# An encoder layer on one core: the middle LayerNorm moved beside the gate's first block, the last LayerNorm rewritten for VectorE

## The chip, the cores and the metric

The kernel runs on one core of a Trainium2 chip. A core has five engines that run side by side and wait for each other through semaphores: PE (TensorE, matrix products), DVE (VectorE), ACT (ScalarE), POOL (GpSimd) and SP (SyncE, which here only issues transfers). The metric is the device time of one execution in microseconds. Three executions of the kernel before took 2086.29, 2087.13 and 2090.3 us; the median is 2087.13 us.

## The reference

One layer for 384 tokens (256 of a prompt, 8 x 16 of running streams), model width 2048, all in fp32. Cut to what matters here:

```python
def layer_norm(x, g, b):
    mu = mean(x, -1); var = mean(square(x - mu), -1)
    return (x - mu) * rsqrt(var + 1e-5) * g + b

x = layer_norm(x, ln_in_g, ln_in_b)
mix = concat(forgetting attention, 8 heads; gated delta rule, 8 heads) @ w_out      # 2048 x 2048
x = layer_norm(2 ** 0.25 * x + mix, ln_mix_g, ln_mix_b)                             # the middle LayerNorm
ffn = (silu(x @ w_gate) * (x @ w_up)) @ w_down                                      # d_ff = 5632
y = layer_norm(2 ** 0.25 * x + ffn, ln_ffn_g, ln_ffn_b)                             # the final LayerNorm
```

Outputs are y and the new states of the heads.

## The kernel before, in words

**Tiles.** The 384 tokens are three row tiles of 128 (`TT = 3`). The residual stream `x_res` holds [128 tokens, 3 tiles, 2048]. For a product, PE needs it transposed and split: `aT_hi` and `aT_lo` ([128 channels, 16 channel groups, 384 tokens]) hold a value rounded to fp32r and the rest.

**Weight pieces.** All weights pass in pieces of [128, 512], numbered `g` through the whole program. SP loads a piece to one of 8 slots of `raw`; ACT copies it to `w_hi` (L226), DVE subtracts and gives `w_lo` (L231). These two are rings of 4: a split of piece g waits until PE has used piece g - 4 (`w_used`). A product (`gemm`, L244) takes, for each piece, three tiles of tokens and for each tile three matmuls (hi x hi, hi x lo, lo x hi): 9 matmuls of 128x512. `w_used` of a piece comes with its last matmul on tile 2. ACT and DVE work 3 pieces ahead of PE.

**Stages.** Entry LayerNorm; 8 attention heads; 8 delta-rule heads; `w_out` in 8 blocks of 8 pieces; the middle LayerNorm; the FFN in two halves (gate block of 16 pieces, up block of 16 pieces for 6 and then 5 groups of 512 hidden channels, each half followed by 4 down blocks of 24 or 20 pieces); the final LayerNorm. Order is written out by hand, engine by engine. A `Course` lets small work of one stage stand between the pieces of a product.

**The middle LayerNorm before.** DVE adds the last `w_out` block to `x_res` (L1399), takes statistics (L285), moments (L291) and 1/sqrt by three Newton steps on [128, 3] (L265 to L270). Then come 12 rounds, one for each tile of tokens and quarter of 512 channels: ACT normalises (L307), DVE multiplies by g (L315), POOL adds b (L322), PE transposes four 128x128 blocks (L337), ACT copies them from PSUM to `aT_hi` (L348), DVE subtracts for `aT_lo` (L353). g and b are broadcast to all 128 partitions. The rounds go tile by tile, so the gate's first product can start only after all 12.

**The final LayerNorm before.** After the last down block DVE adds it to `x_res` (L1567), takes statistics and moments, and 12 rounds follow on ACT (L307), DVE (L315) and POOL (L322), each followed by a store of 256 KB. Its g and b are loaded to `raw` once all weights are split.

**Delta-rule heads.** In each head PE issues four small products into two banks (`streams`), two before and two after the products of L1060 and L1062; before the second two it waits for the first two (`g_S01_ps`).

## Time and profile before

| | us |
|---|---|
| median of 3 runs (lowest, highest) | 2087.13 (2086.29, 2090.3) |
| profiled execution, its own time | 2089.48 |
| its span, first to last instruction | 2087.8 |
| PE busy | 1963.7 (94%) |
| DVE busy | 1071.0 (51%) |
| ACT busy | 774.2 (37%) |
| POOL busy | 187.5 (9%) |
| mean granted clock of PE | 0.982 |
| share of PE in the chain of waits | 81% |

Engines overlap, so the shares don't add up. A group's line names engine, source line, operation, out<-in, shapes and count, then busy time and the mean of one instruction in ns. A busy PE isn't PE at its peak: matmuls overlap, and one of 128x512 lasts 0.39 us but follows the one before it by 0.227 us. In the chain of waits each piece was released by the one above it, and "issue" is time in which nothing visible was waited for.

### The profile page before, as it was taken

How to read it: one execution, taken by the hardware profiler on the slowest of the kernel's cores; microseconds unless marked ns; L12 is line 12 of the kernel's file. 1: busy time of each engine (PE TensorE's matmuls, PEld its weight loads, DVE VectorE, ACT ScalarE, POOL GpSimd, SP SyncE). 2: the span in 40 equal slices, each digit the busy share in tenths (PEclk: the TensorE clock that was granted, in tenths of full speed). 3: DMA queues.
4: the chain of work that ended last, by engine and by line, in shares of the span. 5: the costliest groups of instructions: out<-in, count | busy, mean ns of one | idle time of the engine just before them, and what ended most of it. 6: DMA issues, size and time to landing. Idle time of an engine off the chain costs nothing.

```text
span 2087.8 us, 32037 instructions
## 1 busy us (share of the span) xinstructions
PE 1963.7 (94%) x9970; PEld 1634.1 (78%) x9970; DVE 1071.0 (51%) x2274; ACT 774.2 (37%) x1538; POOL 187.5 (9%) x263
## 2 busy tenths in 40 slices
PE   2999999999999998989999999999999999999993
PEld 1899998777777777867888888888888888888882
DVE  7355655677777676455444434343333444444445
ACT  3344443444444443334333333333333333333332
POOL 4011110211222210003000000000000000000003
PEclk9899999999999999998999999999999999999997
DMA  5355555333333332342444444433344444443332
GB/s 171 81 141 143 141 149 134 93 93 98 98 98 98 91 95 76 126 157 81 126 122 131 126 126 125 127 125 129 128 127 131 126 125 124 122 131 126 126 121 101
DMA packets 235946, 249.82 MB, mean 120 GB/s; under 512 B 21624, under 2 KB 154720, under 8 KB 234608
## 3 DMA queue, kind: packets, MB, share of 16 engines
q1 hardware_dynamic: 229376, 235.48, 39.6%
q0 software_dynamic: 6512, 13.60, 2.1%
q8 instruction: 32, 0.52, 0.1%
q14 instruction: 26, 0.21, 0.0%
HBM read 237.63 MB, written 11.35 MB: 119 GB/s over the span
## 4 chain that ended last, share of the span: by engine, by line
PE 81%; DVE 10%; issue 4%; ACT 2%; DMA 1%; POOL 1%; DVEq 0%; POOLq 0%; ACTq 0%; SPq 0%
PE bank L244 71%; DVE work_a L1170 2%; DVE w_lo L231 2%; DMA x_res<-in_x_prompt 1%; ACT w_hi L226 1%; PE bank L1008 1%; POOL x_res L322 1%; PE bank L1502 1%; PE bank L1002 1%; PE bank L1028 1%; DVE x_res L315 1%; DVE pol L267 0%; DVE pol L268 0%; PE bank L436 0%; PE bank L1022 0%
## 5 line engine op out<-in xcount | busy, mean ns | idle before, releaser
L231 DVE TENSOR_TENSOR w_lo<-raw,w_hi 128x512 fp32r<-128x512 f32 x848 | 588.1, 700 | 750.8 <-ACT w_hi L226 747.0
L226 ACT ACTIVATE w_hi<-raw 128x512 fp32r<-128x512 f32 x848 | 526.8, 630 | 835.7 <-PE bank L244 835.5
L244 PE MATMUL bank<-w_hi,aT_hi 128*128 128x512 f32 (+1 forms) x1824 | 721.7, 396 | 8.5 <-DVE w_lo L231 5.8
L244 PE MATMUL bank<-w_hi,aT_lo 128*128 128x512 f32 (+1 forms) x1824 | 694.3, 381 | 0.0
L244 PE MATMUL bank<-w_lo,aT_hi 128*128 128x512 f32 (+1 forms) x1824 | 693.2, 380 | 0.0
L244 PEld LDWEIGHTS bank<-w_hi,aT_hi 128*128 128x128 f32 x1824 | 345.2, 189 | 74.9 <-DVE w_lo L231 16.3
L244 PEld LDWEIGHTS bank<-w_hi,aT_lo 128*128 128x128 f32 x1824 | 344.2, 189 | 57.5
L244 PEld LDWEIGHTS bank<-w_lo,aT_hi 128*128 128x128 f32 x1824 | 345.5, 189 | 47.5
L244 PE MATMUL bank<-w_hi,hT_hi 128*128 128x512 f32 x528 | 206.9, 392 | 0.6 <-DVE x_res L1567 0.5
L244 PE MATMUL bank<-w_hi,hT_lo 128*128 128x512 f32 x528 | 205.9, 390 | 0.0
L244 PE MATMUL bank<-w_lo,hT_hi 128*128 128x512 f32 x528 | 205.8, 390 | 0.0
L322 POOL TENSOR_TENSOR x_res<-x_res,raw 128x512 f32<-128x512 f32 x12 | 19.5, 1658 | 1104.7 <-DVE x_res L315 1104.7
L244 PEld LDWEIGHTS bank<-w_hi,hT_hi 128*128 128x128 f32 x528 | 99.2, 188 | 23.1 <-issue 1.7
L244 PEld LDWEIGHTS bank<-w_hi,hT_lo 128*128 128x128 f32 x528 | 99.2, 188 | 20.8
L244 PEld LDWEIGHTS bank<-w_lo,hT_hi 128*128 128x128 f32 x528 | 99.2, 188 | 20.2
L244 PE MATMUL bank<-w_hi,mixT_hi 128*128 128x512 f32 x192 | 78.8, 410 | 4.9 <-DVE x_res L1399 4.4
L337 PE MATMUL bank<-cn,x_res 128*128 128x128 f32 x96 | 26.5, 432 | 55.5 <-POOL x_res L322 34.5
L244 PE MATMUL bank<-w_lo,mixT_hi 128*128 128x512 f32 x192 | 75.7, 394 | 0.0
L244 PE MATMUL bank<-w_hi,mixT_lo 128*128 128x512 f32 x192 | 75.6, 394 | 0.0
L337 PEld LDWEIGHTS bank<-cn,x_res 128*128 128x128 f32 x96 | 17.2, 217 | 64.4 <-issue 43.4
L1170 DVE SCALAR_TENSOR_TENSOR work_a<-early,cw,work_a 128x384 f32<-128x384 f32 x72 | 44.6, 620 | 20.5 <-POOL early L1298 14.1
L1521 DVE TENSOR_TENSOR hT_lo<-bank,hT_hi 128x512 f32 (+1 forms) x33 | 22.8, 692 | 55.8 <-ACT hT_hi L1513 55.8
(298 smaller groups left out, 1634.7 us busy)
## 6 DMA issues: line engine op xcount, KB each, us to landing
raw<-in_ffn_w_gate SPq DMA_DIRECT2D x176, 256.0 KB, 2.7
raw<-in_ffn_w_up SPq DMA_DIRECT2D x176, 256.0 KB, 2.7
raw<-in_ffn_w_down SPq DMA_DIRECT2D x176, 256.0 KB, 3.0
raw<-in_w_in SPq DMA_DIRECT2D x128, 192.0 KB, 2.4
raw<-in_w_in SPq DMA_DIRECT2D x128, 128.0 KB, 2.2
raw<-in_w_in SPq DMA_DIRECT2D x256, 64.0 KB, 2.2
raw<-in_w_out SPq DMA_DIRECT2D x61, 256.0 KB, 3.0
work_b<-in_cache_fox_k POOLq DMA_DIRECT2D x8, 512.0 KB, 4.4
```

Of the source, the lines that this page charges most:

```text
L226: nc.scalar.activation(w_hi[:, g % RING], raw[:, g % RAW], ACT.Copy).then_inc(sem("w_high"), 1)
L231: nc.vector.tensor_tensor(w_lo[:, g % RING], raw[:, g % RAW], w_hi[:, g % RING], ALU.subtract).then_inc(sem("w_split"), 1)
L244: last = nc.tensor.matmul(acc[t][:, 0:width], l[:, k0 + n, t * P:(t + 1) * P], r[:, g % RING, 0:width], start=(n == 0 and j == 0), stop=(n ...
L315: nc.vector.tensor_tensor(x, x, gb[0][:, c], ALU.mult).then_inc(sem("ln_scaled"), 1)
L322: nc.gpsimd.tensor_tensor(x, x, gb[1][:, c], ALU.add).then_inc(sem("ln_done"), 1)
L337: last = nc.tensor.transpose(bank[6 + r % 2][:, k * P:(k + 1) * P], x_res[:, t, c:c + P], ident)
L1002: nc.tensor.matmul(tl(b4, 0), A[:, 0, :], U[:, 0, :], start=True, stop=True)\
L1008: last = nc.tensor.matmul(tl(b6, t), A[:, t, :], U[:, t, :], start=True, stop=True)
L1028: last = nc.tensor.matmul(tl(b7, t + 1), T[:, t, :], Z[:, t, :], start=True, stop=True)
L1170: ins = V.scalar_tensor_tensor(out=out, in0=ext[:, a, :, r:r + NQ], scalar=w, in1=out, op0=ALU.mult, op1=ALU.add)
L1502: ins = nc.tensor.transpose(bank[6 + t % 2][:, k * P:(k + 1) * P], hb[:, t, k * P:(k + 1) * P], ident)
L1521: nc.vector.tensor_tensor(hT_lo[:, ks, cs], four(bank[6 + t % 2]), hT_hi[:, ks, cs], ALU.subtract).then_inc(sem("h_bank"), 1)
```

## The change

Four parts.

1. **Middle LayerNorm.** The last `w_out` block goes tile by tile in its last 4 pieces (`gemm_tiles_last`), and DVE takes the statistics of each tile as it is added. Only `x * rstd + shift` is then done on `x_res` in place, one quarter of channels for all three tiles at a time: ACT tile 0, DVE tiles 1 and 2. PE transposes that, one channel group of 128 (three tiles) at a time (`turn`). After the transpose a channel is a partition, so g and b are one number per partition (`gb1`, a small load of POOL ahead of the heads), and ACT applies them while it reads PSUM (into `xt`). DVE casts to `aT_hi` and subtracts for `aT_lo`. The gate's first product starts as soon as channel group 0 is there; the other 14 transposes stand in it. Ahead of the first transposes PE issues 6 fp32 products of 128x512 whose result nobody reads.
2. **Residual stream.** The FFN's residual needs `x * g + b` in token layout. POOL does it in 24 operations of 128x512 on quarters, spaced 6 pieces apart from piece 20 on. DVE waits for all of them before the first down block.
3. **Final LayerNorm.** The last down block also goes tile by tile in its last 4 pieces. All is on DVE: `(x - mean) * g` for tile 0 as soon as its moments are there, for the other 8 quarters between the Newton steps, then 12 times `x * rstd + b`, each followed by its store. g and b (2 x 1 MB) are loaded into a buffer of their own during the last four down blocks.
4. **Semaphores.** PE waits in `streams` for `g_S2_ps` (the product of L1062) and no longer for `g_S01_ps`; others are merged.

```diff
+        def gemm_tiles_last(pe, g0, pieces, hi, lo, k0, acc, name, block):
+            def product(n, t):
...
+                if t == TT - 1:
+                    last.then_inc(sem("w_used"), 1)
+                elif n == pieces - 1:
+                    last.then_inc(sem(name + "_done"), 1)
+            for n in range(pieces - RING):
+                for t in range(TT):
+                    product(n, t)
+            for t in range(TT):
+                for n in range(pieces - RING, pieces):
+                    product(n, t)
...
-                    streams(0), streams(1).then_inc(sem("g_S01_ps"), 1)
+                    streams(0), streams(1)
...
-                    W("g_S01_ps")
+                    W("g_S2_ps")
...
-                    sp.wait_ge(sem("g_mix"), HEADS + 1)
-                    load_gb(sp, gb, ln_mix_g[0], ln_mix_b[0])
...
+                    for n, v in enumerate((ln_mix_g, ln_mix_b)):
+                        pool.dma_start(gb1[:, n, :], v[0].rearrange("(k p) -> p k", p=P),
+                                       allow_slow_non_contiguous=True).then_inc(sem("gb1_in"), 16)
...
+                    for t in range(TT):
+                        if t == TT - 1:
+                            split_dve(dve, G_UP0, 0)
+                        out_evac(dve, blk, NCB - 1, t, 1.0)
+                        dve.wait_ge(sem("acc_free"), TT * blk + t + 1)
+                        last = row_stats(t, NCB - 1)
...
+            def ln1_pool(pool):
...
+                    for t in range(TT):
+                        x = ln1_quarter(q, t)
+                        pool_wait(pool, sem("w_used"), G_UP0 + X_WHOLE_AT + X_WHOLE_STEP * (2 * TT * q + t))
+                        nc.gpsimd.tensor_tensor(x, x, gbq[:, 0, :], ALU.mult).then_inc(sem("x_times"), 1)
...
+            def ln1_act(act):
+                for n in range(A_ACT):
+                    split_act(act, G_UP0, n)
...
+                ln1_unit_act(act, 0)
+                for k in range(KD):
+                    act.wait_ge(sem("n1_ps"), k + 1)
+                    if k >= 2:
+                        act.wait_ge(sem("n1_low"), k - 1)
+                    nc.scalar.activation(xt[:, k % 2, :], bank[6 + k % 2][:, 0:TOK], ACT.Identity,
+                                         scale=gb1[:, 0, k:k + 1], bias=gb1[:, 1, k:k + 1]).then_inc(sem("n1_val"), 1)
+                    if k % 4 == 1 and k // 4 + 1 < QUARTERS:
+                        ln1_unit_act(act, k // 4 + 1)
+                    split_act(act, G_UP0 + A_ACT, k)
...
+                for k in range(KD):
+                    dve.wait_ge(sem("n1_val"), k + 1)
+                    nc.vector.tensor_copy(aT_hi[:, k, :], xt[:, k % 2, :]).then_inc(sem("n1_high"), 1)
+                    dve.wait_ge(sem("n1_high"), k + 1)
+                    nc.vector.tensor_tensor(aT_lo[:, k, :], xt[:, k % 2, :], aT_hi[:, k, :], ALU.subtract)\
+                        .then_inc(sem("n1_low"), 1)
+                    split_dve(dve, G_UP0 + 1, k)
...
+                for _ in range(WARM):
+                    nc.tensor.matmul(bank[5][:, :], ident, cn[:, 0:CW], start=True, stop=True)
+                turn(0), turn(1)
+                gemm(pe, G_UP0, NP_IN, aT_hi, aT_lo, 0, CW, ACC, "acc", BLK_MIX, between=Course(turns()),
+                     ready=lambda n: pe.wait_ge(sem("n1_low"), n + 1))
...
+                dve.wait_ge(sem("x_whole"), ROUNDS)
...
+                    if c == 1:
+                        sp.wait_ge(sem("h_ps"), TT * (FB[0] + FB[1]))
+                        load_gb(sp, (gb_last[:, 0, :], gb_last[:, 1, :]), ln_ffn_g[0], ln_ffn_b[0])
...
+                for t in range(TT):
+                    down_evac(dve, 1, c, t, blk)
+                    dve.wait_ge(sem("acc_free"), TT * blk + t + 1)
+                    link(dve, row_stats(t, c))
+                    link(dve, nc.vector.bn_aggr(moments[:, t, :], stats[:, t].rearrange("p a b -> p (a b)")))
+                    if t == 0:
+                        for _ in range(QUARTERS):
+                            centre(*next(units))
...
+                for r in range(ROUNDS):
+                    t, x, cs = quarter(r)
+                    dve.wait_ge(sem("y_centred"), r + 1)
+                    nc.vector.scalar_tensor_tensor(out=x, in0=x, scalar=rstd[:, t:t + 1], in1=gb_last[:, 1, cs],
+                                                   op0=ALU.mult, op1=ALU.add).then_inc(sem("y_whole"), 1)
```

On PE, between the last `w_out` product (`mixT` operands) and the gate's first (`aT` operands), the kernel before has 12 rounds of four transposes (`cn` holds the identity), of which these are the last two:

```order
L337 MATMUL bank<-cn,x_res 128x128 [waits x_low,ln_done]
L337 MATMUL bank<-cn,x_res 128x128 x3
L337 MATMUL bank<-cn,x_res 128x128 [waits x_low,ln_done]
L337 MATMUL bank<-cn,x_res 128x128 x3
```

The changed kernel has there, on the same engine:

```order
L1570 MATMUL bank<-cn 128x512 x6
L1561 MATMUL bank<-cn,x_res 128x128 [waits n1_unit_dve,n1_unit_act]
L1561 MATMUL bank<-cn,x_res 128x128 x2
L1561 MATMUL bank<-cn,x_res 128x128 [waits n1_unit_dve,n1_unit_act]
L1561 MATMUL bank<-cn,x_res 128x128 x2
L248 MATMUL bank<-w_hi,aT_hi 128x512 [waits acc_free,n1_low,w_split]
L248 MATMUL bank<-w_lo,aT_hi 128x512
L248 MATMUL bank<-w_hi,aT_lo 128x512
```

So 6 transposes stand ahead of the product instead of 48, and each piece of it waits for its own channel group (`n1_low`).

On DVE, in the middle LayerNorm, the kernel before alternates the multiplication by g with the subtraction, and no weight split stands between them:

```order
L315 TENSOR_TENSOR x_res<-x_res,work_a 128x512 [waits ln_unit]
L353 TENSOR_TENSOR aT_lo<-bank,aT_hi 128x4x128 [waits x_high]
L315 TENSOR_TENSOR x_res<-x_res,work_a 128x512 [waits ln_unit]
L353 TENSOR_TENSOR aT_lo<-bank,aT_hi 128x4x128 [waits x_high] x4
L231 TENSOR_TENSOR w_lo<-raw,w_hi 128x512 [waits w_high] x16
```

The changed kernel has this for the first two channel groups and the next quarter (L233 is the weight split):

```order
L1544 CAST aT_hi<-xt 128x384 [waits n1_val]
L1546 TENSOR_TENSOR aT_lo<-xt,aT_hi 128x384 [waits n1_high]
L233 TENSOR_TENSOR w_lo<-raw,w_hi 128x512 [waits w_high]
L1544 CAST aT_hi<-xt 128x384 [waits n1_val]
L1546 TENSOR_TENSOR aT_lo<-xt,aT_hi 128x384 [waits n1_high]
L233 TENSOR_TENSOR w_lo<-raw,w_hi 128x512 [waits w_high]
L1519 TENSOR_SCALAR x_res<-x_res,rstd,shift 128x512 x2
```

Each channel group now brings a cast, a subtraction and one split, and every fourth two normalisations besides.

On DVE at the end of the program, the changed kernel has this between the last splits and the last moments (L1670 adds the block, L1783 is the centring):

```order
L1670 SCALAR_TENSOR_TENSOR x_res<-x_res,bank 128x512 [waits acc_done,gb_in]
L310 BN_STATS stats<-x_res 128x6 [waits acc_free]
L1794 BN_AGGR moments<-stats 128x2 [waits dve_chain]
L1783 SCALAR_TENSOR_TENSOR x_res<-x_res,moments,gb_last 128x512 [waits dve_chain]
L1783 SCALAR_TENSOR_TENSOR x_res<-x_res,moments,gb_last 128x512 x3
L1670 SCALAR_TENSOR_TENSOR x_res<-x_res,bank 128x512 [waits acc_done]
```

Before, the three additions stand together, then the three statistics, then the three moments.

## Rows read from the trace of the kernel before

**Rows 1.** Stretches: us, then busy us and count by engine; PEclk, DMA share, GB/s.
```profile
928.00:957.00 29.00, 13.73 (x50) 9.12 (x50) 25.73 (x44) 15.25 (x24) 19.59 (x12) 0.54 0.03 9
957.00:1350.00 393.00, 393.00 (x1762) 325.52 (x1761) 160.48 (x238) 136.60 (x223) 0.00 (x0) 1.00 0.45 126
2053.00:2088.00 35.00, 0.00 (x0) 0.00 (x0) 23.00 (x31) 8.57 (x12) 19.48 (x12) 0.56 0.23 90
```
**Rows 2.** Chain of waits around the middle LayerNorm: start us, us, what.
```profile
928.63 0.69 DVE x_res L1399
...
931.36 0.52 DVE moments L291 x3
...
934.27 0.82 ACT x_res L307
...
954.39 1.27 POOL x_res L322
...
956.82 33.20 PE bank L244 x144
```
**Rows 3.** Timeline of the `w_out` block's end: start us, us, engine, line, [idle before].
```profile
926.16 0.63 ACT L226 ACTIVATE w_hi<-raw 128x512 fp32r<-128x512 f32 x1 [1.41 <-PE bank L244]
927.77 0.39 PE L244 MATMUL bank<-w_hi,mixT_lo 128*128 128x512 f32 x1
```
**Rows 4.** Timeline of PE at the gate's first product.
```profile
956.47 0.78 PE L244 MATMUL bank<-w_hi,aT_hi 128*128 128x512 f32 x1
```
**Rows 5.** Chain of waits: 145 matmuls, four transposes, an fp32 product of 256 columns.
```profile
1059.91 32.87 PE bank L244 x145
...
1159.48 0.44 PE bank L1502 x4
...
111.56 0.43 PE bank L693 x2
```
**Rows 6.** Groups of DVE and ACT by form: count, busy us, mean ns.
```profile
L231 DVE TENSOR_TENSOR w_lo<-raw,w_hi 128x512 fp32r<-128x512 f32 x848 | 588.1, 700 | 750.8 <-ACT w_hi L226 747.0
L1170 DVE SCALAR_TENSOR_TENSOR work_a<-early,cw,work_a 128x384 f32<-128x384 f32 x72 | 44.6, 620 | 20.5 <-POOL early L1298 14.1
L1211 DVE TENSOR_TENSOR early<-early,cn 128x384 f32<-128x384 f32 x8 | 4.5, 558 | 0.3
L773 DVE TENSOR_SCALAR nrep<-ccache 128x128 f32 x7 | 1.5, 220 | 0.0
L307 ACT ACTIVATE x_res<-x_res,shift,rstd 128x512 f32<-128x512 f32 x36 | 27.3, 803 | 41.4 <-DVE shift L296 41.4
L1084 ACT ACTIVATE work_a<-bank,cw 128x384 f32<-128x384 f32 x24 | 14.0, 582 | 0.0
```
**Rows 7.** Timeline of PE in a delta-rule head.
```profile
418.74 0.39 PE L1062 MATMUL bank<-work_a,ke 128*128 128x128 f32 x2
419.06 0.70 PE L1055 MATMUL bank<-work_b,ke 32*128 32x256 f32 x4
```
**Rows 8.** Chain of waits and timeline at the end of the program.
```profile
2053.69 1.89 DVE stats L285 x3
2052.54 0.39 PE L244 MATMUL bank<-w_hi,hT_lo 128*128 128x512 f32 x1
2059.43 18.02 DVE L315 TENSOR_TENSOR x_res<-x_res,raw 128x512 f32<-128x512 f32 x12 [0.96 <-ACT x_res L307]
2060.30 19.48 POOL L322 TENSOR_TENSOR x_res<-x_res,raw 128x512 f32<-128x512 f32 x12 [1104.65 <-DVE x_res L315]
```
**Rows 9.** A stretch at the end, columns as in rows 1.
```profile
2048.00:2052.00 4.00, 4.00 (x19) 3.33 (x18) 0.39 (x1) 0.00 (x0) 0.00 (x0) 1.00 1.00 416
```
**Rows 10.** DMA issues: count, KB each, median us to landing.
```profile
out<-x_res SPq DMA_DIRECT2D x12, 256.0 KB, 2.3
```
**Rows 11.** Timeline of POOL: a load of 2048 short pieces, and its wait in head 0.
```profile
2.31 1.22 POOL L556 DMA_DIRECT2D wg<-in_w_in  x1
370.56 0.11 POOL L1296 MEMSET early<- 128x9 f32 x1 [38.48 <-ACT early L1082]
```

More of the change, by code:

```diff
@@ L234, in gemm @@
         def gemm(pe, g0, pieces, hi, lo, k0, width, acc, name, block, i=0, per=0, blocks_per=0, between=None,
-                 first=False, ends=True, slot0=0):
+                 first=False, ends=True, slot0=0, ready=None):
             for n in range(pieces):
@@ L239, in gemm @@
                 pe.wait_ge(sem("w_split"), g + per * i + 1)
+                if ready is not None:
+                    ready(n)
                 for t in range(TT):
@@ L254, in gemm @@
                 between.upto(None)
+        def gemm_tiles_last(pe, g0, pieces, hi, lo, k0, acc, name, block):
+            def product(n, t):
+                g = g0 + n
+                pe.wait_ge(sem("w_split"), g + 1)
+                if n == 0:
+                    pe.wait_ge(sem(name + "_free"), TT * (block - 1) + t + 1)
+                for j, (l, r) in enumerate(((hi, w_hi), (hi, w_lo), (lo, w_hi))):
+                    last = nc.tensor.matmul(acc[t][:, :], l[:, k0 + n, t * P:(t + 1) * P], r[:, g % RING, :],
+                                            start=(n == 0 and j == 0), stop=(n == pieces - 1 and j == 2))
+                if t == TT - 1:
[8 more added lines that the diff above has]
+                    product(n, t)
         def wait_acc(eng, name, block, t, g_end):
@@ L1383, in gdn_stage_act @@
                         split_act(act, G_OUT_FOX + A_ACT, n)
-                    with act.Fori(0, NCB) as c:
+                    with act.Fori(0, NCB - 1) as c:
                         for n in range(NP_HALF):
                             split_act(act, G_OUT_GDN + A_ACT, n, c, NP_HALF)
+                    for n in range(NP_HALF - A_ACT):
+                        split_act(act, G_OUT_LAST + A_ACT, n)
                 def stats_of_block(dve, c, acc_free):
@@ L1416, in gdn_stage_dve @@
                                 out_evac(dve, 2 * HEADS + c, c, t, ALPHA)
-                    with dve.Fori(0, NCB) as c:
+                    with dve.Fori(0, NCB - 1) as c:
                         for n in range(NP_HALF):
@@ L1421, in gdn_stage_dve @@
                             out_evac(dve, 2 * HEADS + NCB + c, c, t, 1.0)
-                        stats_of_block(dve, c, TT * (2 * HEADS + NCB + 1 + c)).then_inc(sem("x_stats"), 1)
-                    dve.wait_ge(sem("x_stats"), NCB)
+                        stats_of_block(dve, c, TT * (2 * HEADS + NCB + 1 + c))
+                    for n in range(NP_HALF - A_DVE):
+                        split_dve(dve, G_OUT_LAST + A_DVE, n)
+                    blk = 2 * HEADS + 2 * NCB - 1
+                    for t in range(TT):
[4 more added lines that the diff above has]
+                        last = row_stats(t, NCB - 1)
+                    link(dve, last)
                 def gdn_stage_pe(pe):
@@ L1468, in encoder_layer, with ln1_quarter @@
             hT_lo = sb(ctx, "hT_lo", [P, KH, TOK], F32R)
-            sg = sb(ctx, "sg", [P, TT, CW])
-            hb = sb(ctx, "hb", [P, TT, CW])
+            with ExitStack() as hidden:
+                sg = sb(hidden, "sg", [P, TT, CW])
+                hb = sb(hidden, "hb", [P, TT, CW])
+                xt = sb(hidden, "xt", [P, 2, TOK])
+                gbq = sb(hidden, "gbq", [P, 2, CW])
+            gb_last = sb(ctx, "gb_last", [P, 2, D])
+            def ln1_quarter(q, t):
+                return x_res[:, t, q * CW:(q + 1) * CW]
@@ new lines, in ln1_unit_act, with ln1_unit_dve @@
+            def ln1_unit_act(act, q):
+                x = ln1_quarter(q, 0)
+                nc.scalar.activation(x, x, ACT.Identity, scale=rstd[:, 0:1], bias=shift[:, 0:1])\
+                    .then_inc(sem("n1_unit_act"), 1)
+            def ln1_unit_dve(q):
+                for t in (1, 2):
+                    x = ln1_quarter(q, t)
+                    nc.vector.tensor_scalar(x, x, rstd[:, t:t + 1], shift[:, t:t + 1], ALU.mult, ALU.add)\
+                        .then_inc(sem("n1_unit_dve"), 1)
@@ new lines, in ln1_dve @@
+            def ln1_dve(dve):
+                moments_dve(dve, range(TT))
+                dve.wait_ge(sem("ln_moments"), TT + 1)
+                ln1_unit_dve(0)
+                for k in range(KD):
[5 more added lines that the diff above has]
+                    split_dve(dve, G_UP0 + 1, k)
+                    if k % 4 == 1 and k // 4 + 1 < QUARTERS:
+                        ln1_unit_dve(k // 4 + 1)
+                for n in range(1, A_DVE):
+                    split_dve(dve, G_UP0 + NP_IN, n)
@@ new lines, in ln1_pe, with turn, turns @@
+            def ln1_pe(pe):
+                def turn(k):
+                    pe.wait_ge(sem("n1_unit_act"), k // 4 + 1)
+                    pe.wait_ge(sem("n1_unit_dve"), 2 * (k // 4 + 1))
+                    if k >= 2:
+                        pe.wait_ge(sem("n1_val"), k - 1)
+                    for t in range(TT):
+                        last = nc.tensor.transpose(bank[6 + k % 2][:, t * P:(t + 1) * P],
+                                                   x_res[:, t, k * P:(k + 1) * P], ident)
+                    last.then_inc(sem("n1_ps"), 1)
+                def turns():
+                    for k in range(2, KD):
+                        yield SLOTS * (k - 2) + 1
+                        turn(k)
+                for _ in range(WARM):
[3 more added lines that the diff above has]
+                     ready=lambda n: pe.wait_ge(sem("n1_low"), n + 1))
@@ L1634, in ffn_dve @@
                 half(1, G_UP1, FB[0])
-                for c in range(NCB):
+                for c in range(NCB - 1):
                     down_block(1, G_DN1 + c * NP_DN[1], c, end=G_END, course=(
```

106 lines of the change are left out of this document (57 added, 49 removed).

## The prediction

> **What bounds the kernel now.** I read first the busy shares, then the chain of waits, then the stretches around the two places that the change touches. PE is busy in 94% of the span, and the chain lies on it for 81% (table above). In the FFN it never pauses: between 957 and 1350 it is busy for 393 of 393 us at a granted clock of 1.00 [rows 1]. A change can gain only where the chain leaves PE. It does so for long in two places: 928 to 957, where PE is busy for 13.73 of 29 us at a granted clock of 0.54, and from 2053 to the end, where PE does nothing and POOL and DVE share the time [rows 1]. In the first the chain goes DVE, ACT, and then twelve rounds that end in POOL's addition, until the last of these ends at 954.39 + 1.27 = 955.66 [rows 2]. In the second it is POOL's addition again, 12 in 19.48 us, with DVE's multiplication stretched to 18.02/12 = 1.50 us beside it, against 0.70 for a split of the same size [rows 6, 8].
>
> **Middle LayerNorm.** The last `w_out` matmul starts at 927.77 and ends at 928.16 [rows 3]; call this E. The gate's first matmul starts at 956.47 [rows 4], E + 28.3.
>
> In the changed kernel tiles 0 and 1 are ready 24 and 12 matmuls ahead of E (5.4 and 2.7 us), so only tile 2 is left: addition 0.69 [rows 2] and statistics 0.65 (three took 1.89 in rows 8) end at E + 1.4. Before, the moments started at 931.36 = E + 3.2 and the shift was ready at 934.25, 2.9 us later [rows 2]. That chain stays, so the shift is ready at E + 4.3. One quarter is normalised: ACT 0.80 [rows 6], while DVE does two. A DVE tensor_scalar of 512 columns is not in the trace: 0.22 us at 128 columns [rows 6] and 0.70 for a two-input operation at 512 bound it; I take 0.5, so both engines end at about E + 5.3. PE meanwhile runs 6 fp32 products. One of 256 columns took 0.43 us [rows 5], so one of 512 takes 0.86 and six take 5.1 us: they end as the quarter comes. Then three transposes (0.11 each [rows 5], and 0.2 to drain), ACT's read with g and b (0.58 with one pointer operand at 384 columns [rows 6], some 0.67 with two), DVE's cast (between 0.22 and 0.56 [rows 6]; 0.36) and subtraction (0.56 [rows 6]): 2.2 us with the handovers. The first product starts at E + 7.5 = 935.7, 20.8 us earlier.
>
> In it stand 14 turns of three transposes, 14 x 0.34 = 4.8 us of PE's time. A piece then lasts 9 x 0.227 = 2.04 [rows 5] plus 0.34 = 2.38 us. Does the chain that feeds it keep this pace? ACT reads channel group k + 1 only behind the split that waits for the end of piece k - 1. From there: split 0.63 after a matmul's last 0.17, read 0.67, cast 0.36, subtraction 0.56, handovers 0.1, together 2.4 to 2.5 us, for a piece that PE wants 2.38 us later. A miss of d costs d/2 per piece, since the chain spans two. I take 1 us over the block; with a cast of 0.56 it is 2.5. Against that, the product before began at half clock: 144 matmuls took 33.2 us where 144 x 0.227 = 32.6 [rows 2, 5]; 0.5 us comes back. Sum: 20.8 - 4.8 - 1.0 + 0.5 = 15.5 us gained, with 12 to 17.5 as its range.
>
> **PE's clock.** The stretch of the middle LayerNorm shows a granted clock of 0.54, though PE issued 48 transposes there [rows 1]: near 1.2 GHz in place of 2.4. The Trainium skill says why (TensorE: Matmul & The Clock Gate, PE-mode transpose): transposes don't count as PE activity as products do. By that rule, transposes alone would leave the product cold, and the trace agrees. The six fp32 products leave a pause of only some 1.4 us before the gate, so I expect the higher level at its start.
>
> **Residual on POOL.** 24 operations, some 1.6 us each as the twelve in rows 8 (19.48/12), move into the FFN. There DVE has work for 160 of 393 us [rows 1], and a split comes up to 4 us ahead of the piece that needs it (it starts at the end of piece g - 4, needs 1.4 us, and PE comes to g three pieces of 2.04 later). Rows 8 price a collision at 1.50 - 0.70 = 0.8 us. Cover 4 us, price 0.8: nothing. Without cover, 24 x 0.8 = 19 us. The Trainium skill (GPSIMD Engine Reference, Specifications) names the cause, shared SBUF interfaces between GpSimd and a DVE instruction with two SBUF inputs, which every split is; the trace agrees. It speaks against spacing POOL work among splits. The last of the 24 runs at piece 158 of 192, so DVE's wait for them costs nothing. POOL's new load of 2 x 2048 single numbers is issued ahead of the heads: a load of 2048 short pieces took 1.22 us to issue, and POOL then idles 38.48 us [rows 11].
>
> **Heads.** In `streams` PE now waits for the product just ahead. It starts at 418.74 and ends at 419.13, while the next one starts at 419.06 [rows 7]. The next one can start only after 419.15 and has its weights still to load: 0.1 to 0.4 us in each of 8 heads. I take 0.2, so 1.6 us lost, 0 to 3 as range. PE's order is fixed and the product behind it follows, so nothing hides it.
>
> **Final LayerNorm.** The last matmul ends at 2052.54 + 0.39 = 2052.93 [rows 8]; call this F. The last POOL addition starts 12 x 1.66 after 2060.30 and ends at 2079.8 = F + 26.9 [rows 8]; 8 us follow (the last store, 2.3 us to landing [rows 10], and the program's end).
> Now: tile 0 is ready at F - 5.4. Addition, statistics and moments take 0.69 + 0.65 + 0.2 with two waits, 1.6; the four centrings, with two SBUF inputs and a pointer (0.62 at 384 columns [rows 6], so 0.7 to 0.75 at 512), 2.8: F - 1.0. Tiles 1 and 2, 1.6 each: F + 2.2. Eleven small steps of the root, eight with a centring beside it at 0.82 and three at 0.2: 7.2, F + 9.4. Twelve last operations at 0.70: 8.4, F + 17.8. Gain 9.1. The stores now come every 0.7 us in place of 1.66; 256 KB at the 416 GB/s of a full stretch [rows 9] take 0.63, so they nearly keep up; I take 0.6 off. Net 8.5, range 6.5 to 9.5. The g and b load of 2 MB takes 5 us of all DMA engines at that rate, against a lead of 8 pieces (16 us) of the weight loads, so it is hidden.
>
> **Sum.** 15.5 + 8.5 - 1.6 = 22.4 us. The profiled execution took 2089.48, of which 2087.8 is span, and lies 2.35 above the median of 2087.13. So it would be 2067.1 for that execution, and 2064.7 for the median. I forecast 2065.
>
> **Rivals.**
> (a) The chain that feeds the opening block is the bound. Every piece waits for ACT and DVE, whose work between two pieces (split 0.63, read 0.67, every fourth time a normalisation 0.80 on ACT; cast, subtraction, split 0.70 and twice 0.5 on DVE) is 2.1 and 2.6 us at the worst. If they don't overlap as I have it and the step is 3 us, the block takes 16 x 3.0 = 48 in place of 38.4: 10 us of the gain go, 2075. For it: DVE and ACT have next to no slack in the fourth turns. Against: two thirds of the chain is off either engine's own busy time.
> (b) POOL's 24 operations reach PE. If half of them strike a split or an addition that PE waits for at 0.8 us, 10 us go: 2075. Against: 4 us of cover.
> (c) Slower: PE falls to the lower clock in the opening block and stays there, since waits and transposes now break up the products. 144 matmuls at twice 0.227 cost 32.6 us more, against a gain of 22.4: 2097. It decides if the lower level lasts for more than 99 matmuls (22.4/0.227). Against: before, after 28 us at the lower level, the product lost only 0.5 us. It is the one mechanism that could cost more than the whole gain.
> (d) The change does only its end: something in the new middle path (`n1_unit`, the small load of g and b) arrives so late that the first product starts no earlier than before. Gain 8.5 - 4.8 - 1.6 = 2.1: 2085. Nothing in the rows speaks for it.
>
> **Chances.** Forecast with its own range 2061 to 2069: 0.77. (a) 0.10, (b) 0.06, (c) 0.03, (d) 0.02, and 0.02 for something else on the slow side. The bounds of the terms (12 to 17.5, 6.5 to 9.5, -3 to 0) give gains of 15.5 to 27, that is 2060 to 2071.6; the range goes to 2072 to take in part of (a). A measurement of this kernel tells about 0.2%, 4 us, from no change. Faster: forecast, (a), (b) and half of the rest, 0.94. Same 0.02, slower 0.04.
>
> **What would show it.** In the changed profile: the gate's first product starts 7 to 8 us after the last `w_out` matmul, not 28; its 16 pieces take 38 to 40 us with 3 transposes 14 times between them, at a granted clock near 1.00; after it PE is as gapless as before, with POOL's 24 operations beside it; in each head PE pauses 0.1 to 0.4 us at the second pair of `streams`; from the last matmul to the last DVE operation it is 17 to 19 us. I am wrong if the opening block shows waits of PE for the cast or the subtraction of over 0.3 us in most pieces, if its clock is near 0.5, or if DVE's operations at the end last much over 0.75 us.

## The result, and the profile after

The changed kernel took 2059.74 us (median of 4 runs, 2057.01 to 2060.77) where the kernel before took 2087.53 beside it (4 runs, 2086.29 to 2090.3): a ratio of 0.9863, with 0.9846 to 0.988 as its interval. That is 27.8 us less. 22.4 was worked out, and the time lies 0.3 us under the range of 2060 to 2072. The profiled execution took 2060.06 us, of which 2058.5 is span, at a mean granted clock of 0.993 (before: 0.982). Below, "before" and "after" are the two kernels' profiled executions.

I cut the span at events that both traces have, in us from its start:

| | before | after | length before | length after |
|---|---|---|---|---|
| attention heads' first transposes | 108.4 | 106.2 | 108.4 | 106.2 |
| last `w_out` block, last addition starts | 928.6 | 926.0 | 820.2 | 819.8 |
| gate's opening block done (first activation of the FFN) | 988.7 | 974.3 | 60.1 | 48.3 |
| last down block, last addition starts | 2053.0 | 2039.3 | 1064.3 | 1065.0 |
| end of the span | 2087.8 | 2058.5 | 34.8 | 19.2 |

So the middle gave 12 us (11.8) and the end 15 (15.6, less 0.7 that the down blocks took more). In the middle the execution of before is a short one: with the same middle code, the stretch took 60.9 to 61.1 in the executions of experiments 3, 4 and 10. The first row is not the change: its code is the same in all kernels here, and it ended between 102.8 and 110.1 in their profiled executions. It goes with the granted clock: between 80 and 110 us that is 0.77 before, 0.89 after, and 0.94 in experiment 10, where the row is 105.2. So medians of a few executions can differ by 2 or 3 us from this alone. Where I compare single executions below, I count from this row on.

The stretches of after around the middle LayerNorm (columns as in [rows 1]):

```profile
926.00:931.00 5.00, 5.00 (x12) 1.90 (x10) 4.48 (x19) 0.72 (x2) 0.00 (x0) 1.00 0.20 52
931.00:934.00 3.00, 1.13 (x8) 0.88 (x8) 1.56 (x4) 2.17 (x5) 1.19 (x2) 1.00 0.00 1
934.00:938.00 4.00, 4.00 (x13) 3.14 (x13) 2.63 (x6) 0.49 (x1) 0.00 (x0) 0.57 0.81 241
938.00:974.00 36.00, 35.89 (x169) 26.65 (x168) 23.35 (x47) 18.74 (x31) 0.00 (x0) 1.00 0.35 98
974.00:1380.00 406.00, 406.00 (x1827) 336.10 (x1826) 181.20 (x250) 140.79 (x230) 34.21 (x30) 1.00 0.46 131
```

PE works through nearly all of it. Only between 931 and 934 does it stand still for some 2 us, and right after that its granted clock is 0.57 for 4 us. The last row is the FFN with POOL's operations in it: PE is busy for 406 of 406 us, as before [rows 1].

The timeline of PE after, at the place of [rows 3, 4]:

```profile
925.54 0.39 PE L268 MATMUL bank<-w_hi,mixT_lo 128*128 128x512 f32 x1
925.77 5.31 PE L1570 MATMUL bank<-cn 128*128 128x512 f32 x12
931.48 0.85 PE L1561 MATMUL bank<-cn,x_res 128*128 128x128 f32 x6 [0.40 <-DVE x_res L1519]
933.79 0.47 PE L248 MATMUL bank<-w_hi,aT_hi 128*128 128x512 f32 x1 [1.47 <-issue]
```

The gate's first product starts 8.25 us after the last one of `w_out`; before it was 28.70. The gain at this point is 20.45 us, where 20.8 was forecast. (The six fp32 products show as 12 matmuls, two passes each.)

The chain of waits after, in the opening block:

```profile
942.08 0.33 PE bank L1561 x3
942.41 2.09 PE bank L248 x9
944.50 0.33 PE bank L1561 x3
944.83 2.32 PE bank L248 x9
947.15 0.33 PE bank L1561 x3
947.48 2.10 PE bank L248 x9
```

Every second piece takes 2.32 us in place of 2.09. Two pieces with their transposes take 5.07 where PE alone needs 4.82 (experiment 9): this is the miss of the chain that feeds PE.

Its end, as [rows 8] before, from the timeline of after, and what SP waits for there (us in total, times, longest):

```profile
2038.05 0.39 PE L268 MATMUL bank<-w_hi,hT_lo 128*128 128x512 f32 x1
2047.45 8.04 DVE L1812 SCALAR_TENSOR_TENSOR x_res<-x_res,rstd,gb_last 128x512 f32<-128x512 f32 x12
```
```profile
SPq L1815 <- DMA out<-x_res: 2.2, 1, 2.2
SPq L1815 <- PEq L1815: 0.2, 1, 0.2
```

The last matmul ends at F = 2038.44, the last DVE operation at 2055.49 = F + 17.1 (forecast 17.8, before F + 26.9). But 3.0 us follow it to the end of the span, where 8.0 followed before. The prediction had left that piece as it was. The same view of before has the reason:

```profile
SPq L1684 <- PEq L1684: 5.4, 1, 5.4
SPq L1684 <- DMA out<-x_res: 2.0, 1, 2.0
```

After the last store had landed, SP waited another 5.4 us at the end of the program. The trace names PE's queue for it, whose drain had long ended. The instructions of that last line (engine, count, ns min/median/max, first and last start) say who was late, before:

```profile
L1684 PEldq DRAIN  x1: 4267/4267/4267, 2048.7 to 2048.7; - x1
L1684 ACTq DRAIN  x1: 8559/8559/8559, 2058.6 to 2058.6; - x1
L1684 DVEq DRAIN  x1: 10376/10376/10376, 2067.1 to 2067.1; - x1
L1684 POOLq DRAIN  x1: 9630/9630/9630, 2077.9 to 2077.9; - x1
```

and after:

```profile
L1815 POOLq DRAIN  x1: 8511/8511/8511, 1271.2 to 1271.2; - x1
L1815 ACTq DRAIN  x1: 642/642/642, 2030.4 to 2030.4; - x1
L1815 PEldq DRAIN  x1: 4267/4267/4267, 2034.2 to 2034.2; - x1
L1815 DVEq DRAIN  x1: 7807/7807/7807, 2047.7 to 2047.7; - x1
```

Start plus duration gives the end of each. DVE's last drain ends with its last operation (2047.7 + 7.8 = 2055.5). POOL's ended at 2087.5, 7.8 us after its last addition (2079.8 by [rows 8]) and 5.4 us after the last store landed. In the changed kernel POOL has its last operation at 1271 and drains in the middle of the FFN, where nobody waits. This was a reading of one trace, so I tested it first.

### The profile page after: what moved, and what is told of

Same layout as the page of the kernel before. It is cut to its first block, busy times and chain, and to the rows that moved or that the text cites. A ratio compares the mean times of both kernels' runs of the same rounds, so it can differ in the third digit from the quotient of the medians.

```text
span 2058.5 us, 32107 instructions
## 1 busy us (share of the span) xinstructions
PE 1961.1 (95%) x9982; PEld 1627.4 (79%) x9982; DVE 1077.9 (52%) x2301; ACT 761.8 (37%) x1522; POOL 186.1 (9%) x273
## 4 chain that ended last, share of the span: by engine, by line
PE 82%; DVE 11%; issue 3%; ACT 2%; DMA 1%; DVEq 0%; POOL 0%; ACTq 0%; SPq 0%; POOLq 0%
PE bank L248 70%; PE bank L268 3%; DVE work_a L1194 2%; DVE w_lo L233 2%; DMA x_res<-in_x_prompt 1%; ACT w_hi L228 1%; PE bank L1032 1%; PE bank L1605 1%; PE bank L1026 1%; PE bank L1052 1%; DVE pol L293 0%; DVE pol L292 0%; DVE x_res L340 0%; PE bank L1046 0%; PE bank L461 0%
## 5 line engine op out<-in xcount | busy, mean ns | idle before, releaser
L233 DVE TENSOR_TENSOR w_lo<-raw,w_hi 128x512 fp32r<-128x512 f32 x848 | 600.6, 715 | 713.7 <-ACT w_hi L228 708.8
L248 PE MATMUL bank<-w_hi,hT_hi 128*128 128x512 f32 x468 | 183.2, 391 | 0.4 <-DVE x_res L1670 0.3
L248 PE MATMUL bank<-w_hi,hT_lo 128*128 128x512 f32 x468 | 182.2, 389 | 0.0
L248 PE MATMUL bank<-w_lo,hT_hi 128*128 128x512 f32 x468 | 182.1, 389 | 0.0
L248 PEld LDWEIGHTS bank<-w_hi,hT_hi 128*128 128x128 f32 x468 | 87.8, 188 | 20.5 <-DVE x_res L1670 1.3
L248 PEld LDWEIGHTS bank<-w_hi,hT_lo 128*128 128x128 f32 x468 | 87.8, 188 | 18.4
L248 PEld LDWEIGHTS bank<-w_lo,hT_hi 128*128 128x128 f32 x468 | 87.9, 188 | 17.7
L248 PE MATMUL bank<-w_hi,mixT_hi 128*128 128x512 f32 x168 | 69.3, 412 | 4.9 <-DVE x_res L1426 4.4
L1194 DVE SCALAR_TENSOR_TENSOR work_a<-early,cw,work_a 128x384 f32<-128x384 f32 x72 | 44.6, 619 | 20.6 <-POOL early L1322 14.1
L362 PE MATMUL bank<-cn,x_res 128*128 128x128 f32 x48 | 13.1, 428 | 41.7 <-DVE aT_lo L378 22.3
L1616 ACT ACTIVATE hT_hi<-bank 128x512 f32 (+1 forms) x33 | 19.8, 599 | 66.8 <-PE bank L1605 66.8
```

Of the source, the lines that this page charges most:

```text
L233: nc.vector.tensor_tensor(w_lo[:, g % RING], raw[:, g % RAW], w_hi[:, g % RING], ALU.subtract).then_inc(sem("w_split"), 1)
L248: last = nc.tensor.matmul(acc[t][:, 0:width], l[:, k0 + n, t * P:(t + 1) * P], r[:, g % RING, 0:width], start=(n == 0 and j == 0), stop=(n ...
L362: last = nc.tensor.transpose(bank[6 + r % 2][:, k * P:(k + 1) * P], x_res[:, t, c:c + P], ident)
L1194: ins = V.scalar_tensor_tensor(out=out, in0=ext[:, a, :, r:r + NQ], scalar=w, in1=out, op0=ALU.mult, op1=ALU.add)
L1616: nc.scalar.activation(hT_hi[:, bass.ds(4 * i, 4), t * P:(t + 1) * P], four(bank[6 + t % 2]), ACT.Copy).then_inc(sem("h_hi"), 1)
```

## Experiments

Each has its edit against the changed kernel or the kernel before, as said. Medians of the kernel before beside them were between 2087.4 and 2087.7.

**1. A last POOL operation, first try.** Changed kernel with one tiny POOL operation behind the last DVE one, in a new tile.

```diff
+        tail = sb(top, "tail", [P, 1])
...
+                pool_wait(pool, sem("y_whole"), ROUNDS)
+                nc.gpsimd.memset(tail[:], 0.0)
```

> The changed kernel, and one more instruction: when the last of DVE's twelve operations is done, POOL sets a tile of 128x1 to zero. Theory A: an engine is drained after its last instruction, and on POOL this takes 7 to 8 us (before: the drain ended 7.8 us after POOL's last addition, the last store had landed 5.5 us ahead of it). The program then ends some 7.5 us behind this instruction, so 4.5 to 5 us later than the changed kernel, near 2064.5. Rival B: the end of the program is set by the last store and a fixed rest, and the 5 us that the tail lost came from the stores; then there is no change, near 2060.

Measured: 2074.12 us (2073.47 to 2075.74), ratio 0.9936 (0.9922 to 0.995). That is 14 us more than the change, far over what a drain could cost. The profile shows two things: POOL's drain of 7.3 us, beginning at 2064.8, and FFN products 0.233 us apart where they were 0.227. The new tile had moved other tiles by 32 bytes. So I repeated it without a new tile.

**2. The same without a new tile.**

```diff
+                pool_wait(pool, sem("y_whole"), ROUNDS)
+                nc.gpsimd.memset(shift[:], 0.0)
```

> The first experiment again without its new tile: POOL's one late instruction now sets the dead 128x3 tile shift to zero, so no tile moves in memory. In the first run the drain of POOL behind that instruction took 7.3 us as theory A said, but 9 us more came from products that read hT and mixT, 0.233 us apart and not 0.227. Theory A (the drain costs 4.8 us at the end, the new tile of 4 bytes cost the rest): 2064.5, products of hT 0.227 us apart. Rival B (a POOL that waits through the second half of the FFN slows the products): 2074 again, 0.233 us apart.

Measured: 2062.51 us (2061.03 to 2064.14), ratio 0.9883 (0.9868 to 0.9898), 2.8 us over the change in the medians. From the last addition of the last down block to the end it is 23.9 us, against 19.2. From its trace, the timeline of POOL, its last drain, and what SP waits for:

```profile
2051.92 0.10 POOL L1833 MEMSET shift<- 128x3 f32 x1 [783.25 <-DVE x_res L1812]
```
```profile
L1815 POOLq DRAIN  x1: 7296/7296/7296, 2051.9 to 2051.9; - x1
```
```profile
SPq L1815 <- PEq L1815: 4.9, 1, 4.9
SPq L1815 <- DMA out<-x_res: 2.2, 1, 2.2
```

An operation of 0.1 us brings back a wait of 4.9 us. The drain behind this POOL instruction takes 7.3 us and sets the end.

**3. Kernel before, half of the additions on DVE.** The other direction: POOL stops after six of its twelve additions, and DVE does the rest.

```diff
...
                 for r in range(ROUNDS):
                     scale_dve(dve, r, gb_last, 2)
+                    if r >= 6:
+                        dve.wait_ge(sem("ln_scaled"), ROUNDS * 2 + r + 1)
+                        _, x, c = quarter(r)
+                        nc.vector.tensor_tensor(x, x, gb_last[1][:, c], ALU.add).then_inc(sem("ln_last"), 1)
...
-                for r in range(ROUNDS):
+                for r in range(6):
                     shift_pool(pool, r, gb_last, 2)
```

> The kernel before; in the final LayerNorm POOL adds b in the first six rounds and DVE in the last six. Counted from DVE's first multiplication at 2059.43, of which the program's end was 28.4 us away: DVE now takes 6 x 1.5 us beside POOL and 12 x 0.7 us alone, 17.4 us, and POOL is through after 6 x 1.66 + 0.9 = 10.9. Theory A (POOL's drain of 7.3 us set the end): it ends at 18.2, hidden, and 3 us after DVE's last operation, as in the changed kernel, the program ends, at 20.4: 8 us gained, 2079.5. Rival B (8 us follow the last operation whatever engine it is on, the prediction's view): 25.4, 3 us gained, 2084.5.

Measured: 2079.9 us (2076.1 to 2082.62), ratio 0.9951 (0.9937 to 0.9965): 7.8 us less for the same arithmetic. Its timeline of DVE and of POOL, and the drains:

```profile
2061.16 9.93 POOL L322 TENSOR_TENSOR x_res<-x_res,raw 128x512 f32<-128x512 f32 x6 [1105.50 <-DVE x_res L315]
```
```profile
2077.59 0.69 DVE L1685 TENSOR_TENSOR x_res<-x_res,raw 128x512 f32<-128x512 f32 x1
```
```profile
L1691 POOLq DRAIN  x1: 10406/10406/10406, 2068.5 to 2068.5; - x1
L1691 DVEq DRAIN  x1: 728/728/728, 2077.6 to 2077.6; - x1
```

POOL's drain ends at 2078.9, 7.8 us after its last addition again, and now before the last store has landed. The last matmul ended at 2053.80 here, so the last operation ends F + 24.5 (before F + 26.9) and the span 2.7 us later (before 8.0). Of the gain 2.4 us is arithmetic and 5.3 the drain.

**4. The end alone.** The kernel before with the new final LayerNorm, `gemm_tiles_last` for the last down block, and g and b in their own buffer.

```diff
-        halves = raw[:].rearrange("p a c -> p (a c)")
-        gb_last = (halves[:, 0:D], halves[:, D:2 * D])
+            gb_last = sb(ctx, "gb_last", [P, 2, D])
...
+                    if c == 1:
+                        sp.wait_ge(sem("h_ps"), TT * (FB[0] + FB[1]))
+                        load_gb(sp, (gb_last[:, 0, :], gb_last[:, 1, :]), ln_ffn_g[0], ln_ffn_b[0])
```

> The kernel before with only the final LayerNorm, the last down block and the load of its g and b from the changed kernel. Theory A: POOL's drain goes too, the gain is 14.8 us, 2072.7. Rival B (the prediction's 8.5 us holds and the other 6 us lie elsewhere): 2079.

Measured: 2072.58 us (2069.67 to 2074.53), ratio 0.9929 (0.9915 to 0.9942): the end alone gives 15 us. Counted from the attention heads on, its trace is 14.1 us shorter than before's. SP's wait of 5.4 us at the end is gone:

```profile
SPq L1729 <- DMA out<-x_res: 2.1, 1, 2.1
SPq L1729 <- PEq L1729: 0.2, 1, 0.2
```

**5. The middle alone.** The changed kernel with the old end.

```diff
-                gemm_tiles_last(pe, G_DN1 + NP_DN[1] * c, NP_DN[1], hT_hi, hT_lo, 0, ACC, "acc", BLK_DN[1] + c)
+                gemm(pe, G_DN1 + NP_DN[1] * c, NP_DN[1], hT_hi, hT_lo, 0, CW, ACC, "acc", BLK_DN[1] + c)
```

> The changed kernel with the final LayerNorm, the last down block and the load of its g and b as before. By the two traces the end gave 14.8 us and the rest 14.5, of which 2.2 arose ahead of the first attention head, where the change has nothing. Theory A (the 2.2 is a difference of single executions): 2087.5 - 12.3 = 2075. Rival B (it belongs to the change): 2073. Rival C (my prediction's size of the middle, 15.5): 2072.

Measured: 2071.59 us (2069.62 to 2074.82), ratio 0.9923 (0.991 to 0.9937): the middle alone gives 15.9 us. The parts together make 30.8, three more than the whole; with intervals of some 3 us to either side this doesn't contradict it. Part of it can be seen in the profiled executions: between 820 and 832 us the granted clock is 1.00 here and 0.86 before and after, and the stretch from the heads to the last `w_out` addition takes 818.0 us against 820.2 and 819.8. The last `w_out` addition to the gate's opening block done takes 46.7 us here, against 48.3 in after, and its granted clock stays at 1.00 throughout.

**6. ACT reads ahead of its split.** The chain of the opening block goes through ACT's split, behind which stands the read of the next channel group. Here the read goes first.

```diff
-                for k in range(KD):
+                def read(k):
...
+                read(0)
+                for k in range(KD):
+                    if k + 1 < KD:
+                        read(k + 1)
                     split_act(act, G_UP0 + A_ACT, k)
```

> The changed kernel, ACT's order in the opening block turned: the read of channel group k + 1 stands ahead of the split that waits for the end of piece k - 1, and not behind it. Theory A: the chain split, read, cast, subtraction sets the pace (two pieces took 5.07 us where PE needs 4.76), so 14 x 0.155 = 2.2 us go and each piece takes 2.38 us; 2057.5. Rival B: DVE's own load or the transposes' seams on PE set the pace: no change.

Measured: 2056.83 us (2055.24 to 2059.14), ratio 0.9855 (0.984 to 0.987). 2.9 us less than the change in the medians, with intervals that overlap; counted from the attention heads on, 2.3 us less. The stretch from the last `w_out` addition to the opening block's end takes 46.1 us against 48.3, though the clock fell here too (0.56 between 931 and 934). PE is busy in 32.00 of 32 us from 938 to 970, and the pieces take 2.08 us each.

**7. No warm products.**

```diff
-WARM = 6
+WARM = 0
```

> The changed kernel without the six fp32 products ahead of the first transposes. Theory A: PE is then idle for some 5.5 us, falls to the lower clock in every execution, and the opening block runs its first 3 to 4 us at half pace: 1.7 us more than an execution that stays at the higher level, and since the changed kernel falls in part of its executions anyway, 1 us on the median, near 2061. Rival B: the lower level lasts through much of the block, as transposes keep breaking it up, 5 us and more: over 2065.

Measured: 2059.9 us (2058.52 to 2063.89), ratio 0.9866 (0.9851 to 0.9881): no difference in the medians. The trace shows the clock all the same:

```profile
930.00:934.00 4.00, 0.37 (x2) 0.40 (x3) 3.03 (x15) 0.81 (x1) 0.00 (x0) 0.76 0.00 0
934.00:938.00 4.00, 2.84 (x10) 2.18 (x9) 2.69 (x6) 2.45 (x4) 1.20 (x2) 0.50 0.28 85
938.00:942.00 4.00, 4.00 (x12) 3.12 (x12) 1.18 (x3) 0.79 (x2) 0.00 (x0) 0.50 0.53 177
942.00:974.00 32.00, 31.90 (x153) 24.10 (x153) 20.64 (x42) 16.14 (x27) 0.00 (x0) 0.99 0.35 93
```

Without them PE pauses longer, is granted 0.50 (1.2 GHz) from 934 to 942, which is the first 6 us of the gate (its first product starts at 936.30), and the stretch from the last `w_out` addition to the opening block's end takes 49.9 us: 1.6 more than after and 3.2 more than the executions whose clock did not fall. One such difference is too small for the medians to tell.

**8. Filling the pause.** Changed kernel with two more fp32 products while ACT and DVE prepare the first two channel groups.

```diff
                 turn(0), turn(1)
+                for _ in range(2):
+                    nc.tensor.matmul(bank[5][:, :], ident, cn[:, 0:CW], start=True, stop=True)
```

> The changed kernel with two more fp32 products between the second turn of transposes and the gate's first product, in the pause of 1.47 us. Theory A: PE has no pause left, the clock stays at the higher level in the opening block (the changed kernel's profile has 4 us at 0.57), 1.7 us less where it fell, 1 us on the median: 2058.7. Rival B: the pause isn't what lowers the clock, and the products only delay the gate by 0.2 us: 2060.

Measured: 2057.6 us (2054.4 to 2060.15), ratio 0.9855 (0.984 to 0.9871). The granted clock between 934 and 938 is 1.00 where it was 0.57, and the stretch to the opening block's end takes 46.8 us in place of 48.3. The pieces alternate as before. In the kernels with the middle path of the changed one (it and experiments 1, 2, 5, 11 to 14), the clock fell there in 2 of 8 profiled executions, and in experiment 6 as well; the other six took about what this one takes. So a fall costs 1.6 us and comes only sometimes. That filling prevents it is not shown: the two filled executions (this and experiment 9) had none, but neither had six of the nine without filling.

**9. Both.** Experiments 6 and 8 together.

> The read of channel group k + 1 ahead of the split (as in e4_read_first, which took 2056.8) and the two products in the pause. If the two causes are apart, 2056 and an opening block with pieces of 2.38 us at a clock of 1.00 throughout; if they are one, 2056.8.

Measured: 2055.02 us (2052.66 to 2058.35), ratio 0.9842 (0.9828 to 0.9855), the fastest version here: 4.7 us under the change, though the intervals still touch. Its chain of waits:

```profile
942.30 0.33 PE bank L1566 x3
942.63 2.08 PE bank L248 x9
944.71 0.33 PE bank L1566 x3
945.03 2.08 PE bank L248 x9
```

These pieces take 2.08 now, the clock is 1.00 through the opening block, and the stretch takes 44.6 us. PE itself is the bound of the opening block.

**10. The wait in the heads alone.** Kernel before, only `g_S2_ps` in place of `g_S01_ps`.

```diff
-                    streams(0), streams(1).then_inc(sem("g_S01_ps"), 1)
+                    streams(0), streams(1)
...
-                    W("g_S01_ps")
+                    W("g_S2_ps")
```

> The kernel before, only the wait between the two pairs of streams turned from g_S01_ps to g_S2_ps. In the changed kernel's profile the second pair starts 0.45 us after the product ahead and not 0.32, but from the first head to the last no time was lost: both profiles show 401.4 us between them. Theory A: 8 heads x 0.13 = 1 us at most, within the noise, 2087.5 to 2088.5. My prediction's size: 2089.

Measured: 2088.09 us (median of 11) against 2087.69 (median of 15), ratio 1.0002 (0.9993 to 1.0011). The upper bound is 2.3 us; the best value is 0.4. This interval alone would still allow the 1.6 us of the prediction; the traces speak against it. In the trace of after:

```profile
416.52 0.39 PE L1086 MATMUL bank<-work_a,ke 128*128 128x128 f32 x2
416.97 0.70 PE L1079 MATMUL bank<-work_b,ke 32*128 32x256 f32 x4
```

The second pair starts 0.45 us behind the product, where it was 0.32 [rows 7], but from the first head's streams to the last head's it is 401.4 us in both traces. The stretch up to the last `w_out` addition took 820.3 us in this experiment and 820.2 before.

**11. POOL's operations in a burst.** Changed kernel, the 24 without spacing.

```diff
-X_WHOLE_AT, X_WHOLE_STEP = 20, 6
+X_WHOLE_AT, X_WHOLE_STEP = 20, 0
```

> The changed kernel with POOL's 24 operations of the residual one after another from piece 20 on, and not 6 pieces apart. POOL then works without a break for 24 x 1.3 = 31 us and more beside the splits. Theory A: a split comes up to 4 us early, each is slowed by less than 0.9 us per POOL operation, so PE never waits: 2060. Rival B: splits with two SBUF inputs take up to 1.5 us each beside POOL, with ACT's reads in the same piece DVE falls behind PE, and 3 to 10 us are lost.

Measured: 2059.62 us (2058.48 to 2059.91), ratio 0.9863 (0.9848 to 0.9878): the same as spaced. POOL's operations take 1.53 and 1.63 us each then, 1.29 when spaced. A split beside one takes twice its time in after:

```profile
982.45 0.69 DVE L233 TENSOR_TENSOR w_lo<-raw,w_hi 128x512 fp32r<-128x512 f32 x1 [1.35 <-ACT w_hi L228]
984.49 1.33 DVE L233 TENSOR_TENSOR w_lo<-raw,w_hi 128x512 fp32r<-128x512 f32 x1 [1.35 <-ACT w_hi L228]
```

and PE never waits for it: from the first activation of the FFN to the last down addition it is 1065.1 us in the burst and 1065.0 spaced. The price of this collision is 0.64 us, under the 0.8 taken, and the cover was enough, even for 24 in a row.

**12 to 14. Where tiles start.** Experiment 1 had lost some 11 us that no instruction explained. Three kernels with an unused tile and nothing else:

```diff
         nwf = sb(top, "nwf", [P, 1])
+        sb(top, "unused", [P, 1])
```

(`[P, 16]` and `[P, 64]` in the others.) They move the start of the transposed operands `mixT` and `hT` by 32, 64 and 256 bytes; before and after the change it is a multiple of 512. (The expectation of 12 says 4 bytes; in the built program the tiles move by 32.) The tiles ahead of the unused one, `aT` and the weights among them, don't move.

> The changed kernel with an unused tile of 4 bytes per partition ahead of mixT and hT, so these start 4 bytes further on; no instruction differs. Theory A: their address slows the products that load them as weights, 0.233 us apart and not 0.227: 1584 of hT and 576 of mixT, 2160 x 0.0063 = 13.6 us less what the waits hide, 2070 to 2073. Rival B (it was the waiting POOL): 2060.

> As e10_shift_4, but the unused tile has 64 bytes per partition. Theory A (what counts is that a row starts on a multiple of 32 or 64 bytes, not where it lies): 2060, products 0.227 us apart. Rival B (any move of the tiles costs, by the place in memory): 2070 and more.

> As e10_shift_4 and e11_shift_64, whose products of hT were 0.233 us apart, but the unused tile has 256 bytes per partition, so mixT and hT start half a step of 512 bytes further on (in the kernel before and in the changed one every tile that PE reads in the large products starts on a multiple of 512). Theory A (multiples of 512 count, as a row of 128 fp32 weights is 512 bytes): 0.233 us, 2070. Theory B (the step that counts is 256 or 128): 0.227 us, 2060.

| moved by | median (range), us | ratio (interval) | `hT` products apart, us |
|---|---|---|---|
| 0 (changed kernel) | 2059.74 (2057.01 to 2060.77) | 0.9863 (0.9846 to 0.988) | 0.227 |
| 32 bytes | 2073.48 (2067.97 to 2073.89) | 0.9925 (0.9912 to 0.9939) | 0.233 |
| 64 bytes | 2069.2 (2069.08 to 2073.45) | 0.9917 (0.9903 to 0.993) | 0.233 |
| 256 bytes | 2060.21 (2058.02 to 2062.03) | 0.986 (0.9845 to 0.9876) | 0.227 |

Seven matmuls of the same block, moved by 32 bytes:

```profile
2021.76 0.40 PE L269 MATMUL bank<-w_lo,hT_hi 128*128 128x512 f32 x1
...
2022.92 0.40 PE L269 MATMUL bank<-w_hi,hT_hi 128*128 128x512 f32 x1
2023.15 0.40 PE L269 MATMUL bank<-w_lo,hT_hi 128*128 128x512 f32 x1
```

and in after:

```profile
2021.73 0.39 PE L268 MATMUL bank<-w_hi,hT_lo 128*128 128x512 f32 x1
...
2022.86 0.39 PE L268 MATMUL bank<-w_lo,hT_hi 128*128 128x512 f32 x1
2023.09 0.39 PE L268 MATMUL bank<-w_hi,hT_lo 128*128 128x512 f32 x1
```

Six steps take 1.39 us against 1.36. Over the 1584 `hT` matmuls 0.006 us each makes 9.5; from the first activation of the FFN to the last down addition it is 1074.2 us against 1065.0. The stretch with the `mixT` products takes 822.5 against 819.8. These two make up the 11 us of experiment 1. The products of `aT` keep their pace (139 in 31.51 us, 0.227 apart). So 12's theory A held and 13's failed: 64 bytes cost as much as 32. 14's theory B held: a start 256 bytes off a multiple of 512 is as good as one on it. Whether 128 would do was not tried.

## Why the prediction was right and where it failed

- **Start of the gate's first product.** Right in mechanism and size: 20.45 us earlier against 20.8. The pieces of it were too: 0.54 for the normalisation (0.5 taken), 0.66 for ACT's read (0.67), 0.36 and 0.56 for cast and subtraction.
- **The opening block.** Right in mechanism, short in size. The chain misses PE by 0.25 us for two pieces (5.07 against 4.82 of PE's own); with the last pieces this is some 2.2 us over the block, where 1.0 was taken; experiment 9 gives it back (46.8 to 44.6 us). The clock, expected at its higher level from the start, fell for some 3 us in this execution and cost 1.6 more (48.3 against 46.7 us). Middle in all: 11.8 us in this execution, just under the given range of 12 to 17.5; 13.4 in those without the fall, or 14.3 against the 61.0 that the old middle mostly took. 15.5 was worked out.
- **POOL in the FFN.** Right, with the price of a collision a little high (0.64 measured, 0.8 taken): 24 operations beside the splits cost nothing, spaced or in a burst.
- **Heads.** The step "nothing hides it" failed. A handover that is 0.13 us later in the head is not later at its end; 1.6 us was taken, and none was found: 401.4 us over the heads in both traces (experiment 10).
- **The end: the step that failed.** "8 us follow (the last store, 2.3 us to landing, and the program's end)" was carried over as fixed. Of the 8.0 only 2.6 were fixed. 5.4 were POOL's drain, which ended 7.8 us after its last addition and after everything else; with POOL gone from the end, 3.0 follow. The compute part came to 9.8 us against 9.1, the stores cost 0.4, not 0.6, and the drain added 5.4: 14.9 us by the table above, where 8.5 was worked out. Experiments 2 (adding it back), 3 (taking it from the kernel before) and 4 show it. (A slip without effect: the last POOL addition starts at 2078.5 and ends 19.48 us after 2060.30; it doesn't start 12 x 1.66 after it.)
- **Rivals.** (a), the feeding chain as the bound, was real but about a fifth of its price: some 2.2 us over the block, 0.23 to 0.25 on every second piece, not 0.6 on each. (b) did not occur. (c) occurred as a fall of some 3 us, not as a state that stays: from 938 to 1380 the granted clock is 1.00 again. (d) did not occur.

The sum by what the runs show: middle 13.4, end 14.9, heads 0, so 28.3 against 27.8 measured. The two errors of the middle and the heads (-2.1, +1.6) nearly cancelled, by luck, and what is left of the miss is the end: 6.4 us, of which the drain is 5.4. What would have caught it: the trace of before has the wait of SP of 5.4 us at its last line, after the store had landed. I had read the last operation and the span's end, and not what lay between them.

Open: whether the 3 us by which the two parts measured apart exceed the whole are more than scatter and the falls of the clock named in experiment 5; and what decides in which executions the clock falls.

## What to carry to other kernels

Take the tail of a program apart like any other stage: from the last operation of each engine to the end of the span, with the drain of each queue, since the drain that ends last can set the end; work for GpSimd belongs well ahead of it. When an experiment adds a tile, look at where the operands of the large products start before its time is explained. And a chain of two engines that feeds PE in turn is worth a look at its order: issuing the read ahead of the split took the wait away here (2.2 us over the block).

## What the runs showed of the hardware

- **GpSimd's drain.** 7.8, 7.8, 7.3 and 7.2 us after its last instruction (before, experiments 3 and 2, after); VectorE's ends with its last operation.
- **Start of a stationary operand.** In the three kernels of experiments 12 to 14, fp32r matmuls of 128x512 whose stationary operand starts 32 or 64 bytes off a multiple of 512 follow each other by 0.233 us in place of 0.227 (also in experiment 1); 256 bytes off, by 0.227.
- **The clock after a short pause.** After six fp32 products, a pause with six transposes in it and 1.47 us of nothing, the granted clock stayed at 1.00 in six executions and fell to the lower level for some 3 us in two (and in experiment 6). With two more products in the pause it was 1.00 in both executions profiled (experiments 8 and 9), which is too few to tell. The Trainium skill (TensorE: Matmul & The Clock Gate, PE-mode transpose) says that a transpose doesn't count as PE-busy in the same way as a product. No run here separates the transposes from the idle time beside them.
- **An fp32 product of 128x512** shows as two matmuls and takes 0.885 us (5.31 for six).
